# Row sums moved between stages, early DMAs reordered, and a seventh expert unit loaded ahead

## The chip, the cores and the metric

One core of one Trainium2 chip runs the whole network in one launch. The metric is device time in microseconds (us) of one execution, from a median of three runs; lower is better.

## What is computed

Two network blocks, batch 1, 512 tokens of width 1024, all in float32. Cut to what matters here:

```
first block:   x += mix(norm(x) @ w_in) @ w_out          # an RWKV half and a GLA half
               x += MoE(norm(x))                         # 32 experts, ff 512, top 2 of one group
second block:  for l in 0, 1:
                 sh1, sc1, g1, sh2, sc2, g2 = c-vector @ w_mod[l]     # "modulation": 48 columns of 128 features per l
                 x += g1 * mixer_l(norm(x) * (1 + sc1) + sh1)         # l = 0: LRU + Hyena, l = 1: conformer convolution
                 x += g2 * expert_choice_MoE(norm(x) * (1 + sc2) + sh2)   # 16 experts, ff 1024, 64 tokens each
```

The modulation depends on the vector c alone, not on x. So it can be computed at any time before it is used: the sums of layer 0 before the second block begins, those of layer 1 (shift, scale, gate of the conformer and of the last MoE) only after the first expert-choice stage. Each of the 2 x 48 columns (and 16 for the context vector) is one "row sum": 128 rows of 1024 weights (512 KB) come by DMA, VectorE multiplies them with silu(c) and adds up, L430.

## The kernel before

**Stages.** The program is a sequence of blocks with a barrier between them, each with one instruction stream per engine: `project_first` (0 to 212 us), `gla_mixer`, `rwkv_keys`, `rwkv_prepare`, `rwkv_scan`, `rwkv_output` (to 618), then `Residual` with `residual_route_first` and the pass over 32 experts (618 to about 1190), an overflow pass, `EvenInputs.run` (to 1354), `lru_and_filters` and two `hyena_conv` (to 1573), `Residual` with `residual_route_choice` and expert stage c0 (1573 to about 2125), the conformer, `Residual` and expert stage c1 (2273 to about 2825), and the final norm.

**Row sums** (class `Modulation`, L388). SyncE loads the rows into a few buffers in turn (three everywhere before the change) and waits before each reuse for the sum that frees the buffer (`load`, L405). ScalarE computes silu(c) once per use (L416). VectorE takes the sums between other work (`vector`, L421). Before the change: 54 in `project_first`, 37 in `rwkv_scan`, 21 in `EvenInputs.run`, 112 in all. `finish_modulation(1)` (L435, three small VectorE operations) ends `EvenInputs.run`, L2595.

**project_first** (L460). 44 tiles in a list: two 128-column tiles per unit of weights, with narrow ones between. The first eight PSUM banks take x, scaled by the norm and transposed by TensorE with a diagonal matrix (L528); it waits for the squares of all four row blocks, of which ScalarE does two (L569). ScalarE's stream begins with four DMA issues: half of x, the first two weight units, and the 32 columns of the gates, `w_gl` (L562 to L564). SyncE issues, without a wait, the other half of x, the constants, `gw2`, c, one row block, the masks, and the next row blocks (L509 to L515). Then per tile: TensorE multiplies, ScalarE evacuates and splits the next unit into its high part (L332), VectorE interpolates (L646 to L648), subtracts for the low part of unit u+2 (L347, waited for by TensorE as `W.ready`), and does some row sums. How many stand behind each tile is a table written by hand, L504 to L505: `room` weighs a tile, `until` is the running number of sums. Behind tile `z_end + 2` = 20 VectorE also does the work on the GLA gates (L651 to L661): one addition, four scans, one subtraction, in one piece.

**Residual** (L1398) is the start of each MoE stage: `src @ w_out` in eight products (m = 0 to 7) of 24 matmuls, after each of which VectorE adds the result to x (L1577 or L1579), scales it (L1582) and, for odd m, splits weights (L347); TensorE then does the router's scores of product m - 1 (L1518). GpSimd adds up squares (L1509). `sync_ring` (L1456) loads expert units ahead on SyncE's queue:

```
                for i in range(3):
                    load_ahead(sp, i)
                self.W.all_split(sp)
                load_ahead(sp, 3)
                sp.wait_ge(mm_done.sem, self.m0 + KD)
                load_ahead(sp, 4)
                load_ahead(sp, 5)
```

**experts_pass** (L1808). Experts go in groups of four (two pairs), a group's weights are 24 units of 2 MB, 96 units in a stage. A ring of six buffers holds them; SyncE refills a buffer when the last matmul on it is done (`refill`, L1952). TensorE reads the units in L2016 (gate and up) and L2057 (down) and runs the groups in a hardware loop with the last one behind it (L2064).

Of the kernel before, what the change touches and what calls it, by code (L numbers as in the profile page):

```python
# [15 lines left out]
P = 128  # L16
# [36 lines left out]
MOD_EARLY, MOD_SCAN, MOD_EVEN = 6, 27, MOD_COLS  # L53
# [5 lines left out]
RAW_AT, ROUTE_AT = 207072, 170208  # L59
FIRST_W_AT = (RAW_AT, SLOTS_AT[3], SLOTS_AT[4])  # L60
# [144 lines left out]
def build(nc, A, out, vec_at, const_at):  # L205
    ctx = ExitStack()
    with ctx:
# [179 lines left out]

        class Modulation:  # L388
# [3 lines left out]
            def __init__(self, st, tag, jobs, bufs=MOD_BUFS, at=None):  # L392
# [7 lines left out]
                self.here = [signal(f"mod{tag}_here{j}") for j in range(bufs)]  # L400
                self.c_here = signal(f"mod{tag}_c_here")
                self.step = signal(f"mod{tag}_step")
                self.silu = signal(f"mod{tag}_silu")

            def load(self, sp, first=0, end=None):  # L405
                for j in range(self.n_c if first == 0 else 0):
                    at = vec_at["c_2_row"] + (self.c_first + j) * D
                    sp.dma_start(self.c[j][:], A["vectors"][:, at:at + D]).then_inc(self.c_here.sem, 16)
                for u in range(first, len(self.jobs) if end is None else end):
                    l, m, _ = self.jobs[u]  # L410
                    if u >= self.bufs:
                        sp.wait_ge(self.step.sem, u - self.bufs + 1)
                    at = vec_at[f"mod_rows_{l}_{m}"]
                    sp.dma_start(self.buf[:, u % self.bufs], A["vectors"][:, at:at + D]).then_inc(self.here[u % self.bufs].sem, 16)

            def silu_of_c(self, act):  # L416
                act.wait_ge(self.c_here.sem, 16 * self.n_c)
                for j in range(self.n_c):
                    nc.scalar.activation(self.c[j][:], self.c[j][:], ACT.Silu).then_inc(self.silu.sem, 1)

            def vector(self, dve, first, end):  # L421

                for u in range(first, min(end, len(self.jobs))):
                    l, m, which = self.jobs[u]
                    if u == 0:
                        dve.wait_ge(self.silu.sem, self.n_c)
                    dve.wait_ge(self.here[u % self.bufs].sem, 16 * (u // self.bufs + 1))
                    w = self.buf[:, u % self.bufs]
                    to = mod_c if which else mods[l]
                    nc.vector.tensor_tensor_reduce(w, w, self.c[which - self.c_first][:], 1.0, 0.0, ALU.mult, ALU.add, to[:, m:m + 1]).then_inc(self.step.sem, 1)  # L430

            def all_done(self, dve):
                dve.wait_ge(self.step.sem, len(self.jobs))
# [26 lines left out]
        def project_first(W, rows, masks, masks_in, parts, proj, gla_q, gla_k, gla_v, gla_gl, gla_og, sums, back, reset, jobs):  # L460
# [24 lines left out]
            with ExitStack() as st:  # L485
# [17 lines left out]
                M = Modulation(st, "0", jobs)  # L503
                room = [{"rwkv": 3, "qk": 6, "v": 3, "og": 6, "gl": 0, "z": 0, "x": 0}[kind] for _, _, kind, _ in tiles]  # L504
                until = [-(-len(jobs) * sum(room[:i + 1]) // sum(room)) for i in range(len(tiles))]  # L505
# [2836 lines left out]
```

## Time and profile before

| | |
|---|---|
| median of 3 runs | 2856.08 us (2850.71 to 2861.59) |
| the profiled execution, its own time | 2849.98 us |
| its span, first to last instruction | 2848.2 us |
| mean granted TensorE clock | 0.93 of full speed |
| busy: TensorE 86%, VectorE 44%, ScalarE 21%, GpSimd 7% | |
| HBM read | 721.58 MB, 254 GB/s over the span |

Engines are PE (TensorE), DVE (VectorE), ACT (ScalarE), POOL (GpSimd), SP (SyncE); "SPq" and "ACTq" are their sequencers as they issue DMAs. In a timeline a bracket at the end of a row is the idle time of the engine before it and what ended it.

### The profile page before, as it was taken

Reading aid. Unit: us, or ns where it says so; the run is one execution under the profiler, and the core shown is the slowest. Engines: PE = TensorE matmul, PEld = TensorE weight load, DVE = VectorE, ACT = ScalarE, POOL = GpSimd, SP = SyncE. Lnnn points to the kernel's source line nnn. Section 1 sums busy time; section 2 is a strip of 40 time slices with the busy share of each in tenths; the row PEclk is TensorE's granted clock in tenths of the full one; section 3 lists DMA queues with packets and bytes.
Section 4 is the critical chain, followed back from the end, with each engine's and each line's share of the span. In section 5 each row is a group of like instructions: output and inputs, shape, how many; then the busy total and the mean of one; then the engine's idle time right before and its main releaser. Section 6 shows DMA issues by size and latency. Waiting matters only on the chain. (4 is left out here: it accounts for less than half of the span.)

```text
span 2848.2 us, 42554 instructions
## 1 busy us (share of the span) xinstructions
PE 2455.7 (86%) x18560; PEld 1512.3 (53%) x18560; DVE 1263.4 (44%) x2094; ACT 585.4 (21%) x855; POOL 190.2 (7%) x136
## 2 busy tenths in 40 slices
PE   6987399978999999899766988898989789989897
PEld 5775399956454555387224834343437464434343
DVE  5867766654332332388676332112127741112113
ACT  3433411023111111153501211000013330101001
POOL 0000001013000000020142210000000030000000
PEclk9997699988999999999777989999999899999999
DMA  5580123242999999634110559999973147999996
GB/s 198 186 272 13 53 79 103 65 148 92 393 417 416 418 417 414 257 122 141 38 45 0 205 237 427 428 428 427 427 313 89 47 191 298 426 428 428 428 427 255
DMA packets 121306, 725.86 MB, mean 255 GB/s; under 512 B 11974, under 2 KB 65478, under 8 KB 84103
## 3 DMA queue, kind: packets, MB, share of 16 engines
q1 hardware_dynamic: 90584, 692.64, 60.2%
q10 hardware_dynamic: 30576, 31.07, 3.3%
q8 instruction: 116, 1.90, 0.3%
q14 instruction: 30, 0.25, 0.0%
HBM read 721.58 MB, written 2.10 MB: 254 GB/s over the span
## 5 line engine op out<-in xcount | busy, mean ns | idle before, releaser
L2016 PE MATMUL ps<-s_ring,s_c_XG 128*64 128x512 f32 x2048 | 472.1, 617 | 83.5 <-DMA s_ring<-in_exp_w 62.1
L2016 PEld LDWEIGHTS ps<-s_ring,s_c_XG 128*64 128x64 f32 x2048 | 164.0, 142 | 385.6 <-issue 384.5
L2128 DVE TENSOR_TENSOR s_c_hid<-ps,s_c_sil 128x512 f32<-128x512 f32 x32 | 34.4, 1073 | 516.0 <-PE ps L2016 516.0
L2057 PE MATMUL ps<-s_ring,s_c_hidT 128*64 128x512 f32 x1024 | 223.6, 594 | 0.1
L2016 PE MATMUL ps<-s_ring,s_m_XG 128*64 128x512 f32 x1024 | 222.9, 593 | 0.0
L2016 PEld LDWEIGHTS ps<-s_ring,s_m_XG 128*64 128x64 f32 x1024 | 72.8, 137 | 142.7 <-issue 141.6
L2057 PEld LDWEIGHTS ps<-s_ring,s_c_hidT 128*64 128x64 f32 x1024 | 72.1, 137 | 137.7 <-issue 136.5
L369 PE MATMUL ps<-s_src_part,s_w_hi_at 128*128 128x512 f32 x384 | 126.0, 410 | 0.6 <-DVE s_src_part L1566 0.6
L2140 DVE SCALAR_TENSOR_TENSOR s_c_Y_lo<-ps,s_c_w_slot,s_c_Y_hi 128x512 fp32r<-128x512 f32 x32 | 22.5, 746 | 211.8 <-ACT s_c_Y_hi L2097 211.8
L2057 PE MATMUL ps<-s_ring,s_m_hidT 128*64 128x512 f32 x512 | 113.4, 595 | 0.0
L369 PE MATMUL ps<-s_h_part,s_w_hi 128*128 128x512 f32 x336 | 105.9, 397 | 6.3 <-DVE s_w_lo L347 6.3
L2128 DVE TENSOR_TENSOR s_m_hid<-ps,s_m_sil 128x512 f32<-128x512 f32 x16 | 17.4, 1087 | 190.3 <-PE ps L2016 190.3
L369 PE MATMUL ps<-s_even_part,s_w_hi_at 128*128 128x512 f32 x320 | 98.7, 390 | 0.0
L1946 DVE SCALAR_TENSOR_TENSOR s_xT<-ps,s_mod_l,s_xT 128x512 f32<-128x512 f32 x144 | 96.0, 739 | 1.8 <-PE ps L1938 1.8
L1944 DVE TENSOR_TENSOR s_xT<-ps,s_xT 128x512 f32<-128x512 f32 x136 | 82.9, 678 | 1.7 <-PE ps L1938 1.7
L2091 ACT ACTIVATE s_c_hidT<-ps 128x512 f32<-128x512 f32 x32 | 17.4, 596 | 321.0 <-PE ps L2033 321.0
L369 PEld LDWEIGHTS ps<-s_src_part,s_w_hi_at 128*128 128x128 f32 x384 | 74.1, 198 | 15.8 <-issue 0.7
L369 PE MATMUL ps<-s_src_part,s_w_lo_at 128*128 128x512 f32 x192 | 77.5, 404 | 0.0
L369 PEld LDWEIGHTS ps<-s_h_part,s_w_hi 128*128 128x128 f32 x336 | 63.5, 191 | 21.1 <-issue 8.1
L430 DVE CUSTOM_DVE_ANT_0 s_mod_w<-s_mod_w,s_mod_silu 128x1024 f32<-128x1024 f32 x54 | 65.2, 1222 | 20.9 <-DMA s_mod_w<-in_vectors 20.5
L369 PE MATMUL ps<-s_cf_part,s_w_hi_at 128*128 128x512 f32 x224 | 71.7, 401 | 0.0
L347 DVE TENSOR_TENSOR s_w_lo_at<-s_w_raw_at,s_w_hi_at 128x2048 fp32r<-128x2048 f32 x28 | 64.0, 2289 | 16.3 <-ACT s_w_hi_at L332 16.3
(634 smaller groups left out, 4421.0 us busy)
## 6 DMA issues: line engine op xcount, KB each, us to landing
s_ring<-in_exp_w SPq DMA_DIRECT2D x192, 2048.0 KB, 17.3
s_ring<-in_moe_w_gate SPq DMA_DIRECT2D x32, 2048.0 KB, 12.1
s_ring<-in_moe_w_up SPq DMA_DIRECT2D x32, 2048.0 KB, 15.2
s_ring<-in_moe_w_down SPq DMA_DIRECT2D x32, 2048.0 KB, 12.6
s_mod_w_at<-in_vectors SPq DMA_DIRECT2D x58, 512.0 KB, 4.3
s_mod_w<-in_vectors SPq DMA_DIRECT2D x54, 512.0 KB, 4.6
s_w_raw<-in_w_in ACTq DMA_DIRECT2D x13, 1024.0 KB, 6.5
s_w_raw_at<-in_w_in ACTq DMA_DIRECT2D x8, 1024.0 KB, 5.9
```

Of the source, the lines that this page charges most:

```text
L347: nc.vector.tensor_tensor(self.lo[:, i % 2, :, at], self.raw[:, i % 2, :, at], self.hi[:, i % 2, :, at].bitcast(F32), ALU.subtract).then_i ...
L369: last = nc.tensor.matmul(bank, w[a][:, i % 2, k, c0:c0 + P], x[b][:, k, at], start=start, stop=stop)
L430: nc.vector.tensor_tensor_reduce(w, w, self.c[which - self.c_first][:], 1.0, 0.0, ALU.mult, ALU.add, to[:, m:m + 1]).then_inc(self.step.se ...
L1944: ins = nc.vector.tensor_tensor(xT[:, d, :], ps[:, bank, :], xT[:, d, :], ALU.add)
L1946: ins = nc.vector.scalar_tensor_tensor(xT[:, d, :], ps[:, bank, :], out_gate(d), xT[:, d, :], ALU.mult, ALU.add)
L2016: last = nc.tensor.matmul(ps[x * SLOTS:(x + 1) * SLOTS, bank + fh, :], XG[:, k, c0:c0 + SLOTS], w[x][:, at:at + 512], start=(k == 0), stop ...
L2057: last = nc.tensor.matmul(ps[rows, DOWN + half, :], hidT[:, f, rows], w[x][:, at:at + 512], start=(f == 0), stop=(f == nj - 1))
L2091: nc.scalar.activation(hidT[:, fh * 4:(fh + 1) * 4, :], ps[:, fh, :].rearrange("p (f s) -> p f s", f=4), ACT.Copy).then_inc(act_did.sem, 1)
L2128: nc.vector.tensor_tensor(hid_out[:, fh * per:(fh + 1) * per, :], ps[:, UP + fh, :].rearrange("s (p j) -> s p j", j=nj), sil[:, fh * 512:( ...
L2140: nc.vector.scalar_tensor_tensor(Y_lo[:, at], ps[:, DOWN + half, :], w_slot[:], Y_hi[:, at].bitcast(F32), ALU.mult, ALU.subtract).then_inc ...
```

## The change

1. `project_first` does 48 row sums instead of 54. `room` is zero for tiles 20 to 23, so no sums stand there. The scans move from tile 20 to tiles 21 and 22 (two each), the subtraction to tile 23.
2. SyncE waits for the first weight unit to land before it issues `gw2` and what follows; `w_gl` moves from ScalarE's queue to SyncE's, behind the first row block.
3. `rwkv_scan` does as many row sums as before, of other rows (37). 8 go to the `Residual` of the first MoE, 8 to that of c0, 11 stay in `EvenInputs.run` (21 before). In a `Residual` they have two buffers, one (for m = 6 two) stands behind each product m = 0 to 6, and the loads stand between those of the expert units. `finish_modulation(1)` moves behind VectorE's first gather in expert stage c0.
4. In c0 and c1 a seventh unit (index 6) is loaded ahead, into a place of its own; the first group is written out ahead of the loop on TensorE, and the refills of the first group go one unit further. Scratch tensors of `residual_route_choice` move to make room.

The semaphores of `Modulation` become shared counters (`Since`). The diff, cut to its core:

```diff
-MOD_EARLY, MOD_SCAN, MOD_EVEN = 6, 27, MOD_COLS
+MOD_SCAN, MOD_ROUTE, MOD_EVEN = 21, 29, 40
+ROUTE_MOD_AT = {"mod_w": 192768, "mod_silu": (200960,)}
+EXTRA_AT = (192768, 223456)
...
                 room = [{"rwkv": 3, "qk": 6, "v": 3, "og": 6, "gl": 0, "z": 0, "x": 0}[kind] for _, _, kind, _ in tiles]
+                room[z_end + 2:z_end + 6] = [0, 0, 0, 0]
...
                         sp.dma_start(vec[:], A["vectors"][:, 0:n_vec]).then_inc(*inputs_in.up(16))
+                        sp.wait_ge(raw_in[0].sem, W.here[0])
                         sp.dma_start(gw2[:], A["gla_gw2"]).then_inc(small_here.sem, 16)
                         M.load(sp, 0, 1)
+                        sp.dma_start(w_gl[:], w[:, :, gl0:gl0 + 32]).then_inc(small_here.sem, 16)
                         sp.dma_start(masks[:], masks_in).then_inc(small_here.sem, 16)
...
                         W.load(act, 0, 2)
-                        act.dma_start(w_gl[:], w[:, :, gl0:gl0 + 32]).then_inc(small_here.sem, 16)
...
                             if i == z_end + 2:
                                 dve.wait_ge(gates.sem, 1)
                                 vlink(nc.vector.tensor_tensor(flat(back), flat(back), flat(sums), ALU.add))
-                                for d in range(2):
-                                    way = slice(None, None, -1) if d else slice(None)
-                                    for c in range(2):
-                                        ins = nc.vector.tensor_tensor_scan(...)
+                            if i in (z_end + 3, z_end + 4):
+                                d = i - z_end - 3
+                                way = slice(None, None, -1) if d else slice(None)
+                                for c in range(2):
+                                    ins = nc.vector.tensor_tensor_scan(...)
                                 vlink(ins)
+                            if i == z_end + 5:
                                 blocks = [x.rearrange("p c (b i) -> p (c b) i", i=GLA_SUB) for x in (back, sums)]
...
+        SIDE_AT = [(0, 1), (1, 2), (2, 3), (3, 4), (4, 5), (5, 6), (6, 8)]
...
+                self.side = Modulation(None, side, 2, (ROUTE_MOD_AT["mod_w"], ROUTE_MOD_AT["mod_silu"])) if side else None
...
-            def sync_ring(self, sp, load_ahead):
+            def sync_ring(self, sp, load_ahead, more=False):
+                M = self.side
+                if M is not None:
+                    M.load(sp, 0, 2)
                 for i in range(3):
                     load_ahead(sp, i)
+                if M is not None:
+                    M.load(sp, 2, 5)
                 self.W.all_split(sp)
                 load_ahead(sp, 3)
+                if M is not None:
+                    M.load(sp, 5)
                 sp.wait_ge(mm_done.sem, self.m0 + KD)
                 load_ahead(sp, 4)
                 load_ahead(sp, 5)
+                if more:
+                    if M is not None:
+                        sp.wait_ge(*M.step.at(len(M.jobs)))
+                    load_ahead(sp, 6)
...
                 for u in range(2, self.n_u):
                     W.load_unit(act, u)
+                if self.side is not None:
+                    self.side.silu_of_c(act)
...
                     if m % self.per == self.per - 1:
                         W.split_lo_unit(dve, m // self.per + 2)
+                    if self.side is not None and m < KD - 1:
+                        self.side.vector(dve, *SIDE_AT[m])
...
+            def slot(i, first_group):
+                if extra is None:
+                    return i % RING
+                if first_group and i <= RING:
+                    return i if i < RING else None
+                return (i - 1) % RING
+
+            def refilled_by(j, first_group):
+                if extra is None or not first_group or j > RING:
+                    return j + RING
+                return j + RING + 1 if j < RING else None
+
+            def pieces(s):
+                if s is None:
+                    return [(extra[0][:], 0, 3072), (extra[1][:], 3072, 4096)]
+                return [(ring[s][:], 0, 4096)]
...
-                        with pe.Fori(0, n_groups - 1) as g:
+                        if extra is not None:
+                            group(0, False, True)
+                        with pe.Fori(0 if extra is None else 1, n_groups - 1) as g:
                             group(g, False)
                         group(n_groups - 1, True)
...
                         M.all_done(dve)
-                        finish_modulation(1)
...
-project_first(..., [(0, m, 0) for m in range(MOD_COLS)] + [(1, m, 0) for m in range(MOD_EARLY)])
+project_first(..., [(0, m, 0) for m in range(MOD_COLS)])
...
+                R = Residual(f"c{l}", ..., side=[(1, m, 0) for m in range(MOD_EVEN, MOD_COLS)] if l == 0 else None)
-                run(Region(ROUTE_AT), None, load_also)
+                run(Region(ROUTE_AT), (lambda: finish_modulation(1)) if l == 0 else None, load_also)
```

## Rows read from the trace of the kernel before

**Rows 1.** Windows of 50 us in the three expert stages; columns as the header says.
```profile
core 0: us, PE busy (x) PEld busy (x) DVE busy (x) ACT busy (x) POOL busy (x), PEclk, DMA share, GB/s
750.00:800.00 50.00, 50.00 (x273) 26.07 (x273) 16.47 (x32) 8.01 (x12) 0.00 (x0) 1.00 0.98 412
...
1750.00:1800.00 50.00, 47.32 (x255) 23.35 (x253) 10.59 (x21) 7.11 (x12) 0.00 (x0) 1.00 1.01 427
...
2750.00:2800.00 50.00, 41.12 (x188) 15.46 (x188) 3.39 (x6) 3.06 (x5) 0.00 (x0) 0.97 1.01 426
```

**Rows 2.** Waits of the whole span: us in total, times, longest us.
```profile
PE ps L2016 <- DMA s_ring<-in_exp_w: 62.1, 33, 2.9
...
PE ps L2016 <- issue: 21.4, 10, 2.7
```

**Rows 3.** Windows of 10 us around the start of expert stages c0 and c1.
```profile
1640.00:1650.00 10.00, 0.28 (x3) 0.31 (x4) 9.16 (x18) 5.10 (x7) 6.51 (x5) 0.50 0.00 0
...
1670.00:1680.00 10.00, 10.00 (x50) 3.38 (x48) 0.00 (x0) 1.19 (x2) 0.00 (x0) 1.00 0.97 408
...
2340.00:2350.00 10.00, 0.21 (x3) 0.24 (x3) 9.22 (x18) 5.00 (x7) 6.42 (x5) 0.56 0.00 0
```

**Rows 4.** Line 1869, units 4 and 5 of c0, issued at 1626.9 and 1627.2 us.
```profile
DMA to landing us min/median/max: 8.9/11.2/13.5
```

**Rows 5.** Timeline of ACT and its queue, first 21 us: start, us, what.
```profile
5.24 11.36 ACTq L564 DMA_DIRECT2D s_w_gl<-in_w_in  x1
16.63 1.28 ACT L566 ACT_TABLE_LOAD   x1 [16.63 <-issue]
...
18.04 1.04 ACT L569 ACTIVATE s_proj<-s_mix 128x1024 f32<-128x1024 f32 x1
...
20.64 1.89 ACT L332 ACTIVATE s_w_hi<-s_w_raw 128x2048 fp32r<-128x2048 f32 x1
```

**Rows 6.** Timelines of DVE and of PE, the same start.
```profile
20.98 0.69 DVE L633 TENSOR_TENSOR s_first_diag<-s_base,s_first_rstd 128x512 f32<-128x512 f32 x1
...
21.82 9.86 PE L528 MATMUL ps<-s_first_diag,s_mix 128*128 128x128 f32 x64 [21.82 <-DVE s_first_diag L633]
```

**Rows 7.** DMAs: issue to landing; the third is line 313's first, issued at 1.2 us.
```profile
s_mix<-in_x ACTq DMA_DIRECT2D x1, 1024.0 KB, 7.9
...
s_vec<-in_vectors SPq DMA_DIRECT2D x1, 318.5 KB, 9.2
...
DMA to landing us min/median/max: 19.0/19.0/19.0
```

**Rows 8.** Timelines of DVE, PE and ACT around 110 us.
```profile
97.54 4.57 DVE L657 TENSOR_TENSOR_SCAN s_mix<-s_masks,s_mix 128x512 f32<-128x512 f32 x4
...
112.02 2.28 DVE L347 TENSOR_TENSOR s_w_lo<-s_w_raw,s_w_hi 128x2048 fp32r<-128x2048 f32 x1
...
114.45 1.19 PE L369 MATMUL ps<-s_h_part,s_w_hi 128*128 128x512 f32 x2 [4.46 <-DVE s_w_lo L347]
...
110.03 0.60 ACT L592 ACTIVATE s_pad<-ps 128x512 f32<-128x512 f32 x1 [4.84 <-PE ps L369]
...
122.40 0.60 ACT L592 ACTIVATE s_pad<-ps 128x512 f32<-128x512 f32 x1 [6.52 <-PE ps L369]
```

**Rows 9.** Groups of instructions of DVE, 139.4 to 212 us: busy, mean ns, idle before.
```profile
L430 DVE CUSTOM_DVE_ANT_0 s_mod_w<-s_mod_w,s_mod_silu 128x1024 f32<-128x1024 f32 x34 | 41.2, 1224 | 20.9 <-DMA s_mod_w<-in_vectors 20.5
```

**Rows 10.** Timeline of DVE at the end of EvenInputs.
```profile
1353.16 0.20 DVE L437 TENSOR_TENSOR s_mod_l<-s_mod_l,s_vec 128x48 f32<-128x48 f32 x1
```

**Rows 11.** The Residual of c0: DVE, POOL, landing of units 0 to 2, page's row landing.
```profile
1601.31 0.75 DVE L1579 SCALAR_TENSOR_TENSOR s_xT<-ps,s_mod_l,s_xT 128x512 f32<-128x512 f32 x1 [5.12 <-PE ps L369]
...
1603.88 2.87 POOL L1509 TENSOR_TENSOR s_route_total<-s_route_total,s_route_sq 128x512 f32<-128x512 f32 x1 [6.18 <-ACT s_route_sq L1486]
1609.20 1.29 POOL L1509 TENSOR_TENSOR s_route_total<-s_route_total,s_route_sq 128x512 f32<-128x512 f32 x1 [2.45 <-ACT s_route_sq L1486]
...
DMA to landing us min/median/max: 11.5/16.4/21.1
...
s_mod_w_at<-in_vectors SPq DMA_DIRECT2D x58, 512.0 KB, 4.3
```

More of the change, by code:

```diff
@@ L385, in product_pair, with __init__ @@
                 return last
+        mod_here = [signal(f"mod_here{j}") for j in range(MOD_BUFS)]
+        mod_c_here, mod_step, mod_silu = (signal("mod_" + n) for n in ("c_here", "step", "silu"))
         class Modulation:
-            def __init__(self, st, tag, jobs, bufs=MOD_BUFS, at=None):
+            def __init__(self, st, jobs, bufs=MOD_BUFS, at=None):
                 self.jobs, self.bufs = jobs, bufs
@@ L399, in __init__ @@
                     self.buf, self.c = place("mod_w_at", at[0], [P, bufs, D]), [place("mod_silu_at", a, [P, D]) for a in at[1]]
[L400 to L403, printed above, removed]
+                self.here = [Since(mod_here[j]) for j in range(bufs)]
+                self.c_here, self.step, self.silu = Since(mod_c_here), Since(mod_step), Since(mod_silu)
             def load(self, sp, first=0, end=None):
@@ L1868, in load @@
                     src = w[e, :, part * k_per:(part + 1) * k_per, :].rearrange("p k f -> p (k f)")
-                sp.dma_start(unit, src).then_inc(unit_in[i % RING].sem, 16)
+                for unit, a, b in pieces(s):
+                    sp.dma_start(unit, src[:, a:b]).then_inc(extra_in.sem if s is None else unit_in[s].sem, 16)
             def load_ahead(sp, i):
@@ L2056, in group @@
                                                 at = j * D + half * 512
-                                                last = nc.tensor.matmul(ps[rows, DOWN + half, :], hidT[:, f, rows], w[x][:, at:at + 512], start=(f == 0), stop=(f == nj - 1))
+                                                last = nc.tensor.matmul(ps[rows, DOWN + half, :], hidT[:, f, rows], columns(w[x], at), start=(f == 0), stop=(f == nj - 1))
                                     last.then_inc(mm.sem, 1)
@@ L3182, in build @@
                         W = first_weights(first)
-                        project_first(W, rows, mk, A["consts"][:, const_at["base_end"] + 1:], parts, proj, gla_q, gla_k, gla_v, gla_gl, gla_og, mix[:, 0:CT, :], mix[:, CT:2 * CT, :], masks["reset"], [(0, m, 0) for m in range(MOD_COLS)] + [(1, m, 0) for m in range(MOD_EARLY)])
+                        project_first(W, rows, mk, A["consts"][:, const_at["base_end"] + 1:], parts, proj, gla_q, gla_k, gla_v, gla_gl, gla_og, mix[:, 0:CT, :], mix[:, CT:2 * CT, :], masks["reset"], [(0, m, 0) for m in range(MOD_COLS)])
                     gla_mixer(gla_q, gla_k, gla_v, mix[:, 0:CT, :], mix[:, CT:2 * CT, :], gla_og, mix[:, CT:2 * CT, :], masks["both64"])
```

85 lines of the change are left out of this document (49 added, 36 removed).

## The prediction

> **What bounds the kernel now.** No engine bounds the whole; I read it by stages. The windows of the expert stages come first [rows 1]: in the first one TensorE is busy all of the time, in c0 and c1 it is not, while the DMA engines are full at 426 to 428 GB/s. The waits agree [rows 2]: TensorE stood 62.1 us, in 33 pieces, for expert units of c0 and c1, and never for those of the first stage. So c0 and c1 end when their 96 units have come. Next the windows before those stages [rows 3]: between the last unit loaded ahead and the first refill nothing is transferred (0 GB/s at 1640 and at 2340), and at 1670 the stream runs. The start comes third: TensorE's first matmul waits until 21.82 for the diagonal matrix [rows 6], and ScalarE, on whose squares that rests, spends 5.24 to 16.6 on the issue of `w_gl` alone [rows 5]. Fourth, at 110 us TensorE waits 4.46 us for split weights, since VectorE had the gates' scans and some row sums in front of them [rows 8]. Fifth, the end of `project_first`: in the last 72 us VectorE does 34 row sums and stands 20.5 us for their rows [rows 9].
>
> **Part 1, the start.** Half of x lands on ScalarE's queue at 0.7 + 7.9 = 8.6, the vectors at 1.7 + 9.2 = 10.9 [rows 7]. Without the issue ScalarE is free at 5.24; its table load (1.28) fits before 8.6. From the first square to the first matmul it takes 21.82 - 18.04 = 3.78 us [rows 5, 6], so TensorE starts at 8.65 + 3.8 = 12.4; the diagonal then needs the vectors at 11.6, and they are there. Gain 21.8 - 12.4 = **9.4**. The next thing due is the first weight unit. Now it lands at 1.2 + 19.0 = 20.2 [rows 7], just before its split at 20.64 [rows 5], with SyncE's rows, c and masks running beside it. The new wait holds those back, so after 10.9 it runs alone; 1 MB at half to all of 428 GB/s is 2.5 to 5 us more, 13.5 to 16. TensorE transposes for 9.86 us first [rows 6], to 22.3, and split high (1.89), split low (2.28) and the first two low parts of x are done by then even from 16. What stands behind SyncE's wait is `gw2`, c, row 0, `w_gl`, masks and all further rows: about 1.8 MB to the masks, at 428 GB/s and with the second unit beside them landed by 21 to 25. ScalarE asks for them after its second high split, now at 34, then at 24.7. A delay beyond 3 us there would cost. Bounds: if the first unit still came at 20.2, its splits and two low parts would end at about 26 instead of 22.3, gain 5.7; above, 9.5.
>
> **Part 2, the scans.** A tile takes 0.60 + 4.84 = 5.44 us between evacuations; the one over the stall takes 122.40 - 110.03 = 12.37 [rows 8]. The stall thus costs 6.9, more than its 4.46, since TensorE starts slowly behind it: the first pair of matmuls takes 1.19 us, against 5.44 for a whole tile of 24. In the new order VectorE does, per tile 20 to 23, the interpolation (2.1) plus addition (2.3), two scans (2.3), two scans (2.3) and subtraction (2.3), with a split of 2.3 behind tiles 20 and 22 and no sums. That is 22 us against four tiles' 21.8. The split behind tile 22 ends near 106.3 (old time axis) instead of 114.3, and TensorE wants it at 110. By the table the next tiles take 1, 2, 1 sums; the split behind tile 26 comes at 126.5 when TensorE wants it at 126.3, which leaves 0.2. Gain **6.7**, bounds 0 (the stall comes back one unit later) and 6.9.
>
> **The tail keeps pace.** 48 sums instead of 54 looks like 7 us off the stage's end, but `room` moves the rest later: by the table 34 sums stand behind the last `rwkv` tile's split before, and 34 after. They are paced by their rows ((41.2 + 20.9 + splits)/34, about 2 us each, [rows 9]), so the end shifts with VectorE's arrival, by the 9.4 + 6.7 of the start and the scans, and the six omitted sums give nothing of their own. Between the splits of units 11 and 12 stand 7 sums instead of 6; TensorE may wait 2 us there, covered by the 10 us it stands at the end for the last sums.
>
> **Part 3, row sums in other stages.** The scan has 37 before and after: nothing. In `EvenInputs` ten sums (12 us of VectorE) go, beside TensorE's products: nothing; the three small operations at its end [rows 10] stood alone, **0.5** gained, and their new place is in VectorE's wait for the first gate and up products. In the two `Residual`s a sum (1.3) stands behind each product's 0.75 + 0.5 and at most one 2.3 split, while VectorE waits 5.12 of 6.4 us in the tiles without a split [rows 11]: time is there. The rows' DMAs are the point. Rows 0 and 1 go first on SyncE's queue, row 2 behind three expert units. Unit 2 lands 21.1 us after its issue [rows 11], at 1596.3; c and two rows ahead of it make 3.7 us more, row 2 another 1.2: 1601.2. VectorE, in order, stands from 1596.2 to there, sums, and takes product 3 at 1602.4 instead of 1601.3. TensorE asks for its result only behind product 4, at 1607.6: 0 lost. Rows 5 to 7 follow unit 3 and land in time if they take near a lone row's 4.3 us. The table of silu makes ScalarE reload the root's table, 1.28 [rows 5], in its wait of 2 us: 0. Bounds for both stages together: 0 to 3 us lost.
> GpSimd's addition takes 2.87 us beside VectorE's split and 1.29 alone [rows 11]. The Trainium skill ("SBUF — State Buffer", "Who interferes with whom") says that a VectorE instruction with two SBUF inputs contends with a GpSimd one that reads SBUF; a row sum is such a one. By the rule the addition at m = 6 takes 1.6 us more, to 1624.9, and is due at 1627: both ways the sum is the same.
>
> **Part 4, the seventh unit.** Units 4 and 5 land by 1627.2 + 13.5 = 1640.7 [rows 4]; unit 6 follows at once, in the 28 us without transfers, and lands near 1646, long before its use at 1661 + 6 x 3.5 = 1682. The full stream then carries 89 units instead of 90. One is 2.097 MB / 0.428 = **4.9** us, in each of c0 and c1: 9.8. TensorE has 62.1/2 = 31 us of waits per stage to give, so it follows. The written-out first group is a third copy of TensorE's code; the bound of its cost is one longest "issue" wait of 2.7 per stage [rows 2], and where DMA paces, none shows: 0. Bounds per stage 0 and 4.9.
>
> **Sum.** 9.4 + 6.7 + 0.5 + 9.8 = **26.4 us**. The profiled execution took 2849.98 (span 2848.2), so it would take 2823.6. It lies 6.1 under the median of 2856.08; against that I forecast 2829.7.
>
> **Rivals.**
> (a) The start is bound by bytes. The same 16 DMA engines carry the same 8 MB in the first 23 us, and the first product finds its weights or the small tensors as late as now. For it: the first unit landed 0.4 us before its split. Against it: 2.8 MB of rows and masks went ahead of it that the new wait holds back. Saving 17.0: 2839.1. The Trainium skill ("DMA: Bandwidth & Descriptors", "Issuing engines are not separate DMA queues") says that issuing from another engine only saves the sequencer's time, usually small. Here one issue held ScalarE for 11.36 us, so the row speaks against "small".
> (b) The stall of 110 us only moves, to the unit behind tile 26, or the row sums hold the tail where it is. Saving 19.7: 2836.4.
> (c) The seventh unit hastens nothing, since the stream has gaps later. Against it: 426 to 428 in every window. Saving 16.6: 2839.5.
> (d) Two of these together, saving about 10: 2846.
> (e) Slower: rows 5 to 7 in the `Residual`s land like expert units (some 17 us) instead of 4.3. Row 5, issued at 1608, comes at 1625, row 7, issued behind sum 5, at 1644; product 7 is then added at 1645 instead of 1627, 18.1 later, in both stages 36.2. Less the 26.4 that is 9.8 slower: 2865.9. It decides once row 7 lands after 1639 (its sum is due before product 7 at 1626.9, and 13.2 a stage are to be lost). Against it: their queue holds only unit 3 ahead, which has landed by then.
>
> **Chances.** Forecast 0.62, (a) 0.12, (b) 0.11, (c) 0.06, (d) 0.05, (e) 0.04. A measurement here tells about 0.5% (14.3 us) from no change. (a), (b), (c) and the forecast lie beyond it, 0.91, less 0.02 for noise: faster 0.89. (d), half of (e) and the noise: same 0.09; the rest of (e): slower 0.02. Range: the forecast with its bounds (up to 0.5 more at the start, 0.2 in the scans) and the runs' spread of 5 either way begins at 2820; to take in (a) to (c) it ends at 2841.
>
> **What would show it.** First matmul near 12.4 with its ScalarE table load near 5; first unit landed by 16. No wait of TensorE for a split over 1 us between 90 and 120, evacuations 5.44 apart. The stage after it begins near 196 instead of 212.4. Each `Residual` as long as before, scores never waiting. One more load ahead in the gap before c0 and c1, then 428 GB/s, and both stages 4.9 shorter. The prediction is wrong if the first matmul stays after 18, if TensorE stands behind products of a `Residual`, or if c0 and c1 keep their length from first gather to end.

## The result, and the profile after

The changed kernel took 2835.04 us in the median, the kernel before 2856.08 beside it: ratio 0.9929, 95% interval 0.9903 to 0.9955. (One of its runs, at 4272 us with the granted clock at 0.549, was disturbed and is left out.) Measured again, with more runs of both, the ratio was 0.9936 (0.9921 to 0.9951). The kernel before came to 2851.3 over all 26 runs of the last comparison, so its first median was a high draw: the change saves about 0.0064 x 2851 = 18 us, and not the 26.4 of the forecast. The time lies inside the forecast's range and 5 us above the forecast. As a ratio the forecast saving would be 0.9908: inside the interval of the first comparison, just outside that of the second.

**The start.** Timelines of ACT with its queue, PE and SP's queue; they answer to [rows 5, 6].

```profile
5.40 1.28 ACT L571 ACT_TABLE_LOAD   x1 [5.40 <-issue]
8.79 1.06 ACT L574 ACTIVATE s_proj<-s_mix 128x1024 f32<-128x1024 f32 x1 [1.89 <-DMA s_mix<-in_x]
13.38 1.91 ACT L334 ACTIVATE s_w_hi<-s_w_raw 128x2048 fp32r<-128x2048 f32 x1 [1.87 <-DMA s_w_raw<-in_w_in]
...
12.59 9.21 PE L534 MATMUL ps<-s_first_diag,s_mix 128*128 128x128 f32 x64 [12.59 <-DVE s_first_diag L638]
21.56 0.70 PE L386 MATMUL ps<-s_h_part,s_w_hi 128*128 128x512 f32 x2
...
13.38 0.34 SPq L517 DMA_DIRECT2D s_gw<-in_gla_gw  x1
14.70 0.43 SPq L519 DMA_DIRECT2D s_w_gl<-in_w_in  x1
```

The table load stands at 5.40 instead of 16.63. TensorE begins at 12.59 instead of 21.82, and ScalarE splits the first unit, landed, from 13.38. It did not run alone: SyncE's rows wait for it, but ScalarE's second unit, issued at 1.78, landed at 16.54 beside it. The first product follows without a gap.

**The scans.** Timelines of DVE and of ACT around 100 us, and PE's row at 165.6; they answer to [rows 8].

```profile
85.36 2.29 DVE L658 TENSOR_TENSOR s_mix<-s_mix 128x2048 f32<-128x2048 f32 x1
89.80 2.33 DVE L663 TENSOR_TENSOR_SCAN s_mix<-s_masks,s_mix 128x512 f32<-128x512 f32 x2
94.29 2.28 DVE L349 TENSOR_TENSOR s_w_lo<-s_w_raw,s_w_hi 128x2048 fp32r<-128x2048 f32 x1
96.49 2.33 DVE L663 TENSOR_TENSOR_SCAN s_mix<-s_masks,s_mix 128x512 f32<-128x512 f32 x2
...
101.75 0.60 ACT L597 ACTIVATE s_pad<-ps 128x512 f32<-128x512 f32 x1 [4.84 <-PE ps L371]
107.19 0.60 ACT L597 ACTIVATE s_pad<-ps 128x512 f32<-128x512 f32 x1 [3.89 <-PE ps L371]
112.64 0.60 ACT L597 ACTIVATE s_pad<-ps 128x512 f32<-128x512 f32 x1 [4.84 <-PE ps L371]
118.08 0.60 ACT L597 ACTIVATE s_pad<-ps 128x512 f32<-128x512 f32 x1 [3.04 <-PE ps L371]
...
165.63 0.70 PE L371 MATMUL ps<-s_h_part,s_w_hi 128*128 128x512 f32 x2 [2.75 <-DVE s_w_lo L349]
```

The wait near 110 us is gone, and the evacuations there are 5.44 apart, as forecast. Another one stands 60 us later, 2.75 us for a later split, where the kernel before has none; it is the one of 2 us that the prediction allowed for.

**The end of project_first.** The group of VectorE's row sums from 123 to 197 us, then the last lines of ACT and DVE in that stage and DVE's first of the next; [rows 9].

```profile
L433 DVE CUSTOM_DVE_ANT_0 s_mod_w<-s_mod_w,s_mod_silu 128x1024 f32<-128x1024 f32 x34 | 41.1, 1224 | 21.4 <-DMA s_mod_w<-in_vectors 21.2
```
```profile
189.30 0.60 ACT L615 ACTIVATE s_gla_og<-ps 128x512 f32<-128x512 f32 x1 [4.84 <-PE ps L371]
...
195.39 1.23 DVE L433 CUSTOM_DVE_ANT_0 s_mod_w<-s_mod_w,s_mod_silu 128x1024 f32<-128x1024 f32 x1 [0.52 <-DMA s_mod_w<-in_vectors]
196.66 0.21 DVE L440 TENSOR_TENSOR s_mod_l<-s_mod_l,s_vec 128x48 f32<-128x48 f32 x1
197.77 1.23 DVE L1309 TENSOR_TENSOR s_g_kc<-s_mix 128x1024 f32<-128x1024 f32 x1 [0.62 <-DVEq L510]
```

34 sums stand in the tail, as before. TensorE's last tile is evacuated at 189.9, the last sum ends at 196.62: VectorE's rows, not TensorE, still set the end of the stage. `gla_mixer` starts at 197.77, in the two profiles of before at 212.53 and 209.78.

**The Residual of c0.** DVE around the third product's result; [rows 11].

```profile
1583.03 0.49 DVE L1605 TENSOR_SCALAR s_cat<-s_xT,s_scaled_l 128x512 f32<-128x512 f32 x1
1592.68 1.23 DVE L433 CUSTOM_DVE_ANT_0 s_mod_w_at<-s_mod_w_at,s_mod_silu_at 128x1024 f32<-128x1024 f32 x1 [9.16 <-DMA s_mod_w_at<-in_vectors]
1593.83 0.75 DVE L1602 SCALAR_TENSOR_TENSOR s_xT<-ps,s_mod_l,s_xT 128x512 f32<-128x512 f32 x1
...
1595.15 1.06 PE L1541 MATMUL ps<-s_route_w,s_cat 128*128 128x16 f32 x8 [0.16 <-DVE s_cat L1605]
1597.22 2.31 DVE L433 CUSTOM_DVE_ANT_0 s_mod_w_at<-s_mod_w_at,s_mod_silu_at 128x1024 f32<-128x1024 f32 x1
```

Row 2 came 29.7 us after the stage's begin at 1562.94 (forecast 28.2) and held VectorE for 9.16 us. TensorE asks for the result so late that it lost 0.16.

**c0 and c1.** PE's waits over the whole span, the landing of the extra unit's four DMAs, and two windows; [rows 1, 2].

```profile
PE ps L2080 <- DMA s_ring<-in_exp_w: 62.5, 35, 3.4
```
```profile
DMA to landing us min/median/max: 14.2/15.4/17.3
```
```profile
1750.00:1850.00 100.00, 88.86 (x430) 37.50 (x428) 12.64 (x18) 9.58 (x16) 0.00 (x0) 0.97 1.01 426
2560.00:2660.00 100.00, 90.53 (x438) 38.05 (x436) 13.58 (x23) 9.58 (x16) 0.00 (x0) 0.97 1.01 428
```

The stream is as full as before, and TensorE waits for as much in total. The extra unit landed at 1631.69, 40 us before its first matmul at 1671.5.

**Stage by stage.** Lengths in us from the traces: to DVE's first instruction of `gla_mixer`; from there to the first MoE; `lru_and_filters` and both `hyena_conv`; c0 and c1 from first gather to last scatter; the conformer between. The first seven kernels have no seventh unit, the others have it. The names are those of the experiments below.

```
                to gla  ..to MoE 1  lru+hyena     c0   conformer     c1    span
before           212.5     406.1      216.6     475.3    145.7     477.9  2848.2
before_again     209.8     405.6      216.5     478.2    149.6     478.0  2852.2
before_scans     213.2     404.7      218.4     475.4    149.2     478.0  2848.7
before_48        205.7     411.4      222.2     477.1    145.9     477.9  2849.2
before_start     201.6     406.8      222.2     477.5    145.4     478.0  2845.1
undo_seventh     195.8     403.1      216.5     478.2    149.6     478.0  2831.9
peel_only        196.4     409.5      221.9     478.1    148.3     477.3  2840.0
changed kernel   197.8     407.4      221.8     471.8    149.4     474.9  2833.4
after_again      196.6     411.3      216.7     471.7    149.4     474.4  2830.8
undo_start       208.0     404.1      216.9     471.6    149.4     474.5  2836.4
undo_scans       194.9     406.0      220.4     471.7    149.6     474.6  2830.3
undo_side        197.8     408.6      221.9     473.9    151.3     473.7  2831.6
tail_40          186.0     404.5      216.8     472.2    147.3     474.3  2812.3
tail_40_scans    190.2     402.6      218.8     471.7    149.6     474.6  2815.0
```

Three of these columns (to MoE 1, lru+hyena, conformer) hold hardly anything that the change touches, and they move by 6 to 9 us over the profiles. In the columns "to gla", c0 and c1 the groups stand apart: that is where the change acts.

### The profile page after: what moved, and what is told of

It reads as the page before. It is cut to its first block and busy times, and to the rows that moved or that the text cites. A ratio compares the mean times of both kernels' runs of the same rounds, so it can differ in the third digit from the quotient of the medians.

```text
span 2833.4 us, 42510 instructions
## 1 busy us (share of the span) xinstructions
PE 2466.3 (87%) x18560; PEld 1514.8 (53%) x18560; DVE 1266.7 (45%) x2094; ACT 593.0 (21%) x861; POOL 192.1 (7%) x136
## 5 line engine op out<-in xcount | busy, mean ns | idle before, releaser
L2080 PE MATMUL ps<-s_ring,s_c_XG 128*64 128x512 f32 x2016 | 471.7, 617 | 76.8 <-DMA s_ring<-in_exp_w 62.5
L433 DVE CUSTOM_DVE_ANT_0 s_mod_w_at<-s_mod_w_at,s_mod_silu_at 128x1024 f32<-128x1024 f32 x64 | 84.5, 1332 | 22.2 <-DMA s_mod_w_at<-in_vectors 22.2
```

What stands on the lines that cost most here:

```text
L2080: last = nc.tensor.matmul(ps[x * SLOTS:(x + 1) * SLOTS, bank + fh, :], XG[:, k, c0:c0 + SLOTS], columns(w[x], at), start=(k == 0), stop=(k ...
```

## The experiments

Each ratio is to the kernel before, run beside it on the same chip, with its 95% interval.

**after_again**: no edit.

> The changed kernel once more, unchanged. Theory A (half-clock pieces fall at random in the stages that the change doesn't touch): the time from first to last product of the stretch between EvenInputs and the second expert-choice Residual (lru_and_filters, the two hyena_conv, the conformer), which took 8.5 us longer than in the kernel before, differs by several us from the first profile of the changed kernel, and the parts gained (start 9.2, scans 6, c0 3.6, c1 4.2) stay within 1 us. Theory B (the change costs these 8.5 us each time): the same stretch is as long as in the first profile, within 1 us. Ratio to the kernel before by A: 0.990 to 0.993; by B: 0.993 to 0.996.

Ratio 0.9936 (0.9921 to 0.9951). `lru+hyena` took 216.7 us where the first profile has 221.8 and the conformer 149.4 again; the stretch before the first MoE took 3.9 us more. Theory A holds for the first; c0 and c1 stayed within 0.5 us, as it says. The ratio itself lies in theory B's range (0.993 to 0.996), so the gain is smaller than theory A had it. The conformer waited for a second profile of before.

**undo_start**, from the changed kernel:

```diff
-                        sp.wait_ge(raw_in[0].sem, W.here[0])
-                        sp.dma_start(w_gl[:], w[:, :, gl0:gl0 + 32]).then_inc(small_here.sem, 16)
...
                         W.load(act, 0, 2)
+                        act.dma_start(w_gl[:], w[:, :, gl0:gl0 + 32]).then_inc(small_here.sem, 16)
```

> The changed kernel with its start as before: w_gl again on ScalarE's queue, no wait of SyncE for the first unit. Step sum: first product at 31.4 instead of 21.6, so 9.8 us longer than the changed kernel (ratio about 0.996 to the kernel before), and nothing of it given back at the end of project_first. Rival (the last row sums of project_first are paced by their rows from a fixed time on): the loss shrinks to under 5 us by the start of gla_mixer.

`gla_mixer` starts at 208.0, 11 us later than in the changed kernel's profiles (mean 197.2): the rival, that the tail swallows it, falls. Ratio 0.9949 (0.9936 to 0.9962), only 3.7 us above after_again, with intervals that overlap. In its profile the stretch from there to the first MoE is 3 and 7 us shorter than in the two of the changed kernel; that stretch scatters as much by itself.

**undo_scans**, from the changed kernel (the old place of the scans is in the diff ahead):

```diff
-                room[z_end + 2:z_end + 6] = [0, 0, 0, 0]
...
-                            if i in (z_end + 3, z_end + 4):
-                                d = i - z_end - 3
...
+                                for d in range(2):
```

> The changed kernel with the four scans and the subtraction in one piece behind tile 20 and the row sums by the old weights (still 48 of them). Step sum: the wait of TensorE near 100 us for the split is back (4 to 5 us), evacuations 12 us apart once, 6 us longer than the changed kernel at tile 28. With 48 sums and none of them moved later, fewer sums (31 by the table, about 3 less than in the changed kernel) stand in the tail. If the tail is paced by rows at 2 us each, it gives all of that 6 us back and gla_mixer starts at the same time within 1 us; if the end shifts with the arrival of VectorE as my prediction said, gla_mixer starts 5 to 7 us later.

Ratio 0.9922 (0.9909 to 0.9936): no slower than the changed kernel. TensorE's wait is back, with 2.85 us instead of the 4 to 5 expected, the one near 165 us is gone, and the stage ends at 194.9, earlier than in all five profiles with the scans moved and 48 sums (195.8 to 197.8). Timelines of PE and DVE of this kernel:

```profile
104.29 0.91 PE L371 MATMUL ps<-s_h_part,s_w_hi 128*128 128x512 f32 x2 [2.85 <-DVE s_w_lo L349]
...
194.91 1.23 DVE L1306 TENSOR_TENSOR s_g_kc<-s_mix 128x1024 f32<-128x1024 f32 x1 [0.30 <-PEq L509]
```

The step of the prediction that gave the scans 6.7 us falls with this.

**undo_seventh**, from the changed kernel:

```diff
-... shift, [place("extra_unit", at, [P, n]) for at, n in zip(EXTRA_AT, (3072, 1024))])
+... shift)
-                    R.sync_ring(sp, load_ahead, True)
+                    R.sync_ring(sp, load_ahead)
```

> The changed kernel with six units loaded ahead and no written-out group. Step sum: c0 and c1 each 4.9 us longer than in the changed kernel, by its trace 3.6 and 4.2; ratio to the changed kernel 1.003. Rival (the seventh unit is worth nothing, since the first group has other waits): both stages as long as in the changed kernel within 1 us.

Ratio 0.9952 (0.9936 to 0.9968). c0 is 6.5 us longer (478.2 against 471.7 and 471.8), c1 3.1 and 3.6. The rival falls. In the whole time it is 4.6 us against after_again's 0.9936, with intervals that overlap.

**before_again**: the kernel before, no edit, one execution.

> The kernel before once more, unchanged, for a second profile of it. All five profiles with the change in whole or part take 3.8 us more than the first profile of before from the end of c0 to the conformer's first products. If that is an accident of the first profile of before (its clock was full there), this profile shows the longer stretch too, 27.5 + 3.8 = 31.3 us; if the change causes it, 27.5 again.

The second profile of before has the longer stretch. The rows are PE's first products of the conformer, in the first profile of before, in the second, and in the changed kernel:

```profile
2130.99 7.03 PE L2930 MATMUL ps<-s_cf_u,s_base 128*1 128x512 f32 x16 [2.90 <-DVE s_cf_u L3069]
```
```profile
2130.94 9.99 PE L2930 MATMUL ps<-s_cf_u,s_base 128*1 128x512 f32 x16 [2.90 <-DVE s_cf_u L3069]
```
```profile
2116.74 9.85 PE L2995 MATMUL ps<-s_cf_u,s_base 128*1 128x512 f32 x16 [2.90 <-DVE s_cf_u L3134]
```

Windows of 7 us there, in the first and in the second profile of before (the column after POOL is the granted clock):

```profile
2131.00:2138.00 7.00, 7.00 (x16) 1.25 (x16) 4.03 (x4) 3.22 (x4) 0.00 (x0) 1.00 0.59 158
```
```profile
2131.00:2138.00 7.00, 7.00 (x10) 1.08 (x11) 3.99 (x4) 3.18 (x4) 0.00 (x0) 0.58 0.62 159
```

The same 16 matmuls take 7.0 us at the full clock, 2.4 GHz, and about 9.9 where most of them fall on a stretch at half of it. That happened in the second profile of before too, so the longer stretch needs no change to appear. Whether the change makes it more frequent is open: the 16 matmuls took 7.0 us in three of the five kernels built from before and in one (tail_40) of the nine built from the changed one. The means of the conformer's column are 147.2 and 149.3.

**before_scans**: the kernel before with the scans' part alone (the `room` line, the scans behind tiles 21 and 22, the subtraction behind 23), 54 sums.

> The kernel before with the scans' part of the change alone: no sums behind tiles 20 to 23, scans behind tiles 21 and 22, subtraction behind 23, still 54 sums. By my prediction: the wait of 4.46 us at 114 us goes and gla_mixer starts 6.7 us earlier. By the new theory (the end of project_first is set by the row sums, 1.95 us each by their rows' loads, and the table moves 4 of them from before tile 27 into the tail): the wait goes too, but gla_mixer starts 0 to 4 us LATER than in the kernel before, and the time is the same or up to 0.1% more.

Ratio 1.0002 (0.9991 to 1.0012). Evacuations, the tail's row sums from 131 us on, TensorE's wait, and the start of `gla_mixer`:

```profile
110.30 0.60 ACT L593 ACTIVATE s_pad<-ps 128x512 f32<-128x512 f32 x1 [4.84 <-PE ps L369]
115.74 0.60 ACT L593 ACTIVATE s_pad<-ps 128x512 f32<-128x512 f32 x1 [3.89 <-PE ps L369]
```
```profile
L430 DVE CUSTOM_DVE_ANT_0 s_mod_w<-s_mod_w,s_mod_silu 128x1024 f32<-128x1024 f32 x38 | 46.0, 1224 | 23.8 <-DMA s_mod_w<-in_vectors 23.6
```
```profile
175.33 1.19 PE L369 MATMUL ps<-s_h_part,s_w_hi 128*128 128x512 f32 x2 [3.60 <-DVE s_w_lo L347]
...
213.22 1.22 DVE L1305 TENSOR_TENSOR s_g_kc<-s_mix 128x1024 f32<-128x1024 f32 x1 [0.30 <-PEq L507]
```

The wait of 4.46 us at 114 has gone, one of 3.60 has come at 175, and nothing is gained. The zeros in `room` push four sums into the tail, 38 instead of 34. At (46.0 + 23.8)/38 = 1.84 us each, more with the splits between, they cost what VectorE's earlier arrival gives (the tail's first sum starts at 133.9 instead of 139.4). TensorE's last tile was evacuated at 201.0, 11 us before the last sum ended: its later wait does not set the end either.

**before_48**: the kernel before with 48 sums in `project_first`.

```diff
-MOD_EARLY, MOD_SCAN, MOD_EVEN = 6, 27, MOD_COLS
+MOD_EARLY, MOD_SCAN, MOD_EVEN = 0, 21, MOD_COLS
```

> The kernel before with 48 sums in project_first instead of 54, nothing else of the change there; the six go to rwkv_scan's list and six of those to EvenInputs (27 there instead of 21). My prediction: the six omitted sums give nothing of their own, gla_mixer starts when it did (223.0 and 220.1 in the two profiles of before, for its first product). New theory: the sums set the end of project_first, so it starts 5 us earlier than their mean of 221.5, at about 216.5, though the wait of 4.46 us at 114 us is still there.

Ratio 0.9974 (0.9962 to 0.9986), 7 us. Row sums of the tail from 139.4 us on, the wait, and the next stage's start:

```profile
L430 DVE CUSTOM_DVE_ANT_0 s_mod_w<-s_mod_w,s_mod_silu 128x1024 f32<-128x1024 f32 x30 | 36.3, 1224 | 15.4 <-DMA s_mod_w<-in_vectors 15.2
```
```profile
115.01 1.19 PE L369 MATMUL ps<-s_h_part,s_w_hi 128*128 128x512 f32 x2 [4.46 <-DVE s_w_lo L347]
...
205.72 1.23 DVE L1302 TENSOR_TENSOR s_g_kc<-s_mix 128x1024 f32<-128x1024 f32 x1 [0.30 <-PEq L506]
```

The wait still stands there, and the stage ends at 205.7 instead of 211.2 (mean of 212.5 and 209.8). The omitted sums pay, not the scans.

**before_start**: the kernel before with the start's part alone, the edit of undo_start the other way.

> The kernel before with the start's part of the change alone (SyncE's wait, w_gl on SyncE's queue). Step sum: first product and the start of gla_mixer 9.4 to 10 us earlier, ratio 0.9966. Rival (what the start gives is given back later, since undo_start came out only 3.7 us above the changed kernel): gla_mixer starts 9 to 10 us earlier but the time is only 3 to 5 us shorter, ratio 0.9986, with the loss in one stage of the profile.

`gla_mixer` starts at 201.6, 9.6 us before that mean. Ratio 0.9974 (0.9961 to 0.9988), so 3.4 to 11 us: it holds the step sum's 9.5 and the rival's upper figure. No stage of the profile gives anything back beyond the scatter of the table. TensorE's wait for the split behind the scans is 2.86 us here, at 104.7, instead of 4.46: the two parts overlap, and with the new start there is less for the scans' move to save.

**undo_side**: the changed kernel with no row sums in the Residuals (`MOD_SCAN, MOD_ROUTE, MOD_EVEN = 21, 21, 48`, no `side`).

> The changed kernel without row sums in the two Residuals: all 16 in EvenInputs (27 there instead of 11), where finish_modulation(1) stays in the first gather of c0. Step sum: the Residuals cost nothing with sums, so they are as long as in the changed kernel within 0.5 us (first product of m1 and of c0 to first gather); EvenInputs, with 16 sums of 1.25 us more in VectorE's idle time, the same within 1.5 us. Rival: sums in the Residuals cost something by the 9 us wait for row 2, then both Residuals are 1 to 3 us shorter here.

Ratio 0.9935 (0.9912 to 0.9957), that of the changed kernel. The first Residual, from its first matmul to the first gather, took 78.0 us, in the changed kernel's two profiles 78.1 and 78.1. That of c0 took 76.7; the profiles with sums there have 78.5 and 79.1, and those of before, without sums, 79.1, 79.2 and (before_48, before_start) 76.7. So 76.7 does not come from leaving the sums out alone: it stands in three of the six profiles without sums there. But none of the eight with sums has it (78.5 to 79.1), so no cost is shown, and one of up to 2.4 us in some executions is not excluded. The stretch between the first MoE's last scatter and `lru_and_filters`, where this kernel has 16 sums more, took 162.0 us, in the changed kernel's profiles 162.4 and 163.6.

**peel_only**: the changed kernel with six units ahead but the first group still written out (`peeled = tag[0] == "c"` in place of `extra is not None` at the loop, and undo_seventh's edit).

> The changed kernel with the first group of c0 and c1 written out ahead of the loop, but six units loaded ahead as before. My prediction: the third copy of TensorE's code costs nothing, so c0 and c1 are as long as in undo_seventh within 1 us. Rival: fetching the copy costs up to 2.7 us a stage, and c0 and c1 are that much longer than in undo_seventh; the seventh unit alone is then worth more than the 4 us a stage that the changed kernel gained.

Ratio 0.9967 (0.9953 to 0.998). The stages are as long as in undo_seventh (478.1 and 477.3), as forecast. The stream of weights inside them is not. From the first to the last landing of the refills:

```
              c0: loads, us, us each    c1: loads, us, us each
before         90   438.0   4.922        90   437.5   4.916
before_again   90   438.0   4.922        90   437.4   4.915
undo_seventh   90   438.0   4.921        90   437.6   4.916
peel_only      90   439.3   4.936        90   439.3   4.936
changed        89   434.4   4.936        89   435.2   4.946
after_again    89   434.3   4.936        89   434.6   4.938
```

Each profile with the third copy has 4.931 or more per unit, each without it 4.922 or less. The DMA queue rows show what came on top, for before and for peel_only:

```profile
q8 instruction: 116, 1.90, 0.3%
```
```profile
q8 instruction: 125, 2.05, 0.3%
```

Nine packets more, of 16 KB; q8 is the queue that brings instructions. Inside each of c0 and c1 the traces of this kernel and of the changed one have twelve of queue q8 where before has eight, each of 1.0 to 1.3 us on one DMA engine; the packets of the weights, equally large, take 0.61. So the copy costs the stream 1.3 to 1.8 us a stage. Most of it falls on one load: where loads land 4.90 apart, one in each stage of peel_only landed 6.19 and 6.09 us after the one before it (at 2021.23 and 2734.97), with a packet of q8 in between (at 2019.08 and 2732.81). undo_seventh has a q8 packet near that place as well (2017.42), and there the load keeps its 4.90; so a packet by itself does not set the price. That the packets are the cause is argued from their times; no run varied them alone. In peel_only the stage ends hide the cost: its last scatter ends 13.6 and 13.4 us after the last landing, in the others 13.6 or some 15. What picks one of the two is not shown; TensorE's granted clock was 1.00 there in before (13.6) and in before_again (15.1).

**tail_40**: the changed kernel with 40 sums in `project_first`.

```diff
-MOD_SCAN, MOD_ROUTE, MOD_EVEN = 21, 29, 40
+MOD_SCAN, MOD_ROUTE, MOD_EVEN = 21, 21, 40
-... masks["reset"], [(0, m, 0) for m in range(MOD_COLS)])
+... masks["reset"], [(0, m, 0) for m in range(MOD_COLS - 8)])
-... side=[(1, m, 0) for m in range(MOD_SCAN, MOD_ROUTE)])
+... side=[(0, m, 0) for m in range(MOD_COLS - 8, MOD_COLS)])
-                        finish_modulation(0)
-                    run(region, lambda: count_overflows(...))
+                    run(region, lambda: (finish_modulation(0), count_overflows(...)))
```

> The changed kernel with 40 instead of 48 sums in project_first: the last 8 columns of layer 0 go to the Residual of the first MoE, and the 8 of layer 1 that stood there to EvenInputs (19 there instead of 11); finish_modulation(0) stands behind VectorE's first gather in that MoE. If the sums set the end of project_first, it ends with the last evacuation instead, at about 188 to 190 us, and gla_mixer starts 6 to 8 us earlier than in the changed kernel; the rest keeps its length; ratio to before about 0.991. If something else holds that end, nothing changes.

Ratio 0.9894 (0.9875 to 0.9913), median 2819.1 us beside 2852.0: the fastest version here with the next one. Last evacuation, last sum and next stage:

```profile
184.35 0.60 ACT L615 ACTIVATE s_gla_og<-ps 128x512 f32<-128x512 f32 x1 [4.84 <-PE ps L371]
...
184.25 1.22 DVE L433 CUSTOM_DVE_ANT_0 s_mod_w<-s_mod_w,s_mod_silu 128x1024 f32<-128x1024 f32 x1 [0.63 <-DMA s_mod_w<-in_vectors]
186.02 1.23 DVE L1308 TENSOR_TENSOR s_g_kc<-s_mix 128x1024 f32<-128x1024 f32 x1 [0.54 <-PEq L510]
```

TensorE and VectorE now end together, 11 us before the changed kernel's stage did. That is more than the 6 to 8 expected. TensorE's wait for a split near 165 us (2.75 and 1.86 in the changed kernel's two profiles) went with the sums, and its last evacuation came at 185.0 instead of 189.9 and 187.4; the wait is part of that, the rest is open.

**tail_40_scans**: tail_40 and undo_scans together.

> As tail_40, and the scans in one piece as in the kernel before. TensorE waits again near 104 us for a split, 2 to 4 us; with the sums out of the way the last evacuation sets the end, so now that wait should show: gla_mixer starts 2 to 4 us later than in tail_40. If the sums still set the end, it starts at the same time or earlier.

The next stage starts at 190.16, 4.1 us later than in tail_40, and TensorE's wait of 3.32 us is back:

```profile
104.60 1.19 PE L371 MATMUL ps<-s_h_part,s_w_hi 128*128 128x512 f32 x2 [3.32 <-DVE s_w_lo L349]
...
189.26 0.60 ACT L614 ACTIVATE s_gla_og<-ps 128x512 f32<-128x512 f32 x1 [4.84 <-PE ps L371]
190.16 1.22 DVE L1305 TENSOR_TENSOR s_g_kc<-s_mix 128x1024 f32<-128x1024 f32 x1 [1.81 <-PEq L509]
```

So the scans' new place is worth about 4 us once TensorE sets the end, and nothing while the sums do. This is one profile of each, and profiles of one kernel differ here by up to 2.7 us (212.5 and 209.8); the returned wait of 3.32 us bears the reading out. In the whole time (0.9891, 0.9872 to 0.9909) 4 us can't be told from tail_40.

## Why the prediction was right, and where it was not

**The start: right.** "Gain 21.8 - 12.4 = 9.4": TensorE began 9.2 earlier, the product after it 9.9, and alone the part moved the stage's end by 9.6. The queue behind the new wait (w_gl, masks) was in time, as forecast. Rival (a) fell. The step "after 10.9 it runs alone" was wrong, since the second unit ran beside the first, but the first came at the early end of 13.5 to 16 all the same. In the whole time the part measured 7.4 us alone and 3.7 in undo_start, both below its 9.6 and 11 at the stage's end, with intervals that reach them or nearly so. No run separates the move of `w_gl` from SyncE's new wait. The Trainium skill ("DMA: Bandwidth & Descriptors", "Issuing engines are not separate DMA queues") calls the time saved on the sequencer usually small relative to the DMA itself; here the issue held ScalarE for 11.36 us in front of the first matmul, and the data landed 18.7 us after the issue began, so it was not small.

**The scans: the step failed.** "Gain 6.7, bounds 0 (the stall comes back one unit later) and 6.9." The gain was 0: 1.0002 alone, and without it the changed kernel is no slower. The stall of 110 us went as described. One of 3.60 us came back, not one unit but 60 us later, in before_scans; in the changed kernel it is 1.8 to 2.8 in the five profiles, and the prediction had it ("TensorE may wait 2 us there, covered"). Neither of them sets the end. Rival (b) named what does, "the row sums hold the tail", and had 0.11. I credited TensorE's stall, though the same text has TensorE standing 10 us at the end of the stage for the last sums: a stall ahead of a wait that long is covered by it. What sets the end is VectorE's arrival and the number of sums behind it. The term was also taken from the stall before the start was changed, 4.46 us; with the new start it is 2.86.

**The tail: right as a count, wrong as a credit.** 34 sums stand behind the last `rwkv` split before and after, and the stage ended near the forecast 196 (197.8 and 196.6). But "the six omitted sums give nothing of their own" is false. Alone they give 5.5 us at the stage's end and 7 in the time; the scans' part takes four sums into the tail and by that uses up its own gain. Both steps together, 6.7 forecast, measure 14.3 - 9.6 = 4.7 at the stage's end (14.3 is 211.2 less the mean, 196.9, of the five profiles with both edits and 48 sums). Two errors of opposite sign nearly cancelled. Rival (b), which had the tail hold the end and gave 2836.4, is the nearest to the measured 2835.04, though the omitted sums pay part of its sum. (a) with 2839.1 and (c) with 2839.5 also lie nearer than the forecast, and the runs refute both: nearness of the total decides nothing here.

**Row sums in the Residuals: right.** Row 2 held VectorE for 9.16 us and TensorE for 0.16; rows 5 to 7 were not late by 17 us, so rival (e) fell. A cost of up to 2.4 us in the time to the first gather is not excluded (undo_side). The 0.5 us of `finish_modulation` can't be seen in the scatter. On GpSimd's additions the trace agrees with the Trainium skill's rule ("SBUF — State Buffer", "Who interferes with whom"): of the eight sums in c0 three took 2.31 us instead of 1.22 beside them, and two additions 2.04 and 2.05 instead of 1.29. At m = 6 that is 0.8 us more and not the 1.6 of the prediction. TensorE waited for neither.

**The seventh unit: right in mechanism, too large in size.** "4.9 us, in each of c0 and c1: 9.8." The refills' stream became 3.6 to 3.7 us shorter in c0 and 2.3 to 2.9 in c1, the stages 5.0 and 3.5 (477.1 to 472.1 and 477.9 to 474.4, means of seven profiles each); in the whole time it is 4.6 to 9 us (0.9936 against undo_seventh's 0.9952 and peel_only's 0.9967). The mis-sized term is "where DMA paces, none shows: 0" for the written-out group. I looked for its price at TensorE, with a bound of 2.7, and it was in the stream that paces the stage, 1.3 to 1.8 us, inside the bound.

**The sum.** Of the parts alone: start 7, omitted sums 7, scans 0, seventh unit about 7, together 21; by stages 14.3 + 8.5 = 22.8; the whole measures 18, interval 14 to 22.5. The 3 to 5 us between stay open: the stages that the change leaves alone scatter by 6 to 9 us from one execution to the next. About 2 us of them may be the conformer's (147.2 and 149.3 on average); what would tie it to the change is not shown. The forecast of 2829.7 was also helped by its base: taken from 2851.3 it would have been 2824.9, further off, if still inside the range. The range's lower end does not follow from its own terms: 2829.7 less 5 for the spread and less 0.7 for the bounds is 2824, not 2820. The measured time lies inside either way.

## What to carry to other kernels

Before a stall is given a price, find what ends the stage: a stall of an engine that stands idle at the stage's end for another one was worth nothing here until that other work was taken away, and then about 4 us. Two parts that act on the same stall don't add up: the new start alone made it 1.6 us shorter. When filler work is dealt out by a table, taking it from one place puts it in another, so count what stands in the tail, not what is gone from the middle. And where transfers pace a stage, look for the price of more code in the stream of transfers as well.

## What the runs showed of the hardware

The time of stages that the change leaves alone goes with TensorE's granted clock. The conformer's first 16 matmuls took 7.0 us at full clock and up to 10.0 with a stretch at half of it. `lru_and_filters` with the convolutions took 216.5 to 216.9 us in the six profiles with a mean granted clock of 0.77 there, and 218.4 to 222.2 in the eight with 0.74 to 0.76, for the same instructions. One profile on either side is therefore not enough to judge 4 us; two of the same kernel show how much a stage moves by itself.

A code packet of 16 KB held a DMA engine for 1.0 to 1.3 us where a weight packet of the same size took 0.61. In a stream at 426 to 428 GB/s, four more of them went with 1.3 to 1.8 us, most of it in one load of 6.1 or 6.2 us instead of 4.9.
